# Prompt attention scored once by query rows, its probabilities transposed in blocks, in quarters of 256 queries

## What is computed

```
def fox_attend(q, fq, pq, k, v, fk, pk):
    s = einsum('bqhd,bkhd->bhqk', q, k) * (HEAD_DIM ** -0.5)
    s = s + swapaxes(fq, 1, 2)[..., :, None] - swapaxes(fk, 1, 2)[..., None, :]
    s = where(pq[:, None] >= pk[None, :], s, -inf)
    p = softmax(s, axis=-1)
    return einsum('bhqk,bkhd->bqhd', p, v)
```

## Time and profile before

| | us |
|---|---|
| median of 3 runs | 733.63 |
| lowest and highest | 733.26, 734.16 |
| the profiled execution | 732.52 |
| its span, first to last instruction | 730.8 |
| PE busy in the span | 690.2 |
| DVE, ACT, POOL busy | 414.1, 243.4, 144.4 |

### The profile page before, as it was taken

One profiled execution on the slowest core, in us unless ns is written; L12 is line 12 of the kernel. 1 busy time (PEld: TensorE's weight loads), 2 busy tenths in 40 slices (PEclk: granted clock), 3 DMA queues, 4 the chain that ended last, 5 costly groups with the idle time before them and its releaser, 6 DMA issues.

```text
span 730.8 us, 12856 instructions
## 1 busy us (share of the span) xinstructions
PE 690.2 (94%) x4958; PEld 545.2 (75%) x4958; DVE 414.1 (57%) x722; ACT 243.4 (33%) x422; POOL 144.4 (20%) x168
## 2 busy tenths in 40 slices
PE   2999999999999999999999998999998999999995
PEld 2789999888888889999999846554554232588884
DVE  4834927472353303179999953536446797455443
ACT  6636442121111345112121233444542384212211
POOL 3044112111111011213121243222320002212210
PEclk9999999999999999999999999999999999999999
DMA  8312103311110032331210687566841050032332
GB/s 256 100 37 59 29 6 67 86 32 30 31 30 2 4 80 93 104 105 30 58 29 1 187 274 252 155 201 190 270 128 54 34 188 1 1 100 73 101 115 87
DMA packets 60757, 67.27 MB, mean 92 GB/s; under 512 B 15188, under 2 KB 50907, under 8 KB 60697
## 3 DMA queue, kind: packets, MB, share of 16 engines
q1 hardware_dynamic: 55529, 51.37, 23.5%
q0 software_dynamic: 5168, 15.08, 6.9%
HBM read 57.71 MB, written 8.68 MB: 91 GB/s over the span
## 4 chain that ended last, share of the span: by engine, by line
PE 70%; DVE 20%; issue 4%; ACT 3%; SPq 2%; DMA 1%; DVEq 0%; ACTq 0%
PE PS L1727 10%; PE PS L1728 8%; PE PS L1729 8%; DVE RA L1403 8%; PE PS L1656 5%; PE PS L1655 5%; PE PS L1657 4%; PE PS L1975 3%; PE PS L1906 3%; PE PS L1992 3%; PE PS L1954 3%; PE PS L2015 3%; DVE rec L1607 2%; DVE wr L1235 1%; DVE RA L1402 1%
## 5 line engine op out<-in xcount | busy, mean ns | idle before, releaser
L1727 PE MATMUL PS<-xh,wh 128*128 128x368 f32 x576 | 202.1, 351 | 0.0
L1728 PE MATMUL PS<-xl,wh 128*128 128x368 f32 x576 | 190.0, 330 | 0.0
L1729 PE MATMUL PS<-xh,wl 128*128 128x368 f32 x576 | 189.7, 329 | 0.0
L558 POOL TENSOR_TENSOR wl<-wr,wh 128x1024 fp32r<-128x1024 f32 x24 | 61.1, 2547 | 312.1 <-ACT wh L913 312.1
L1727 PEld LDWEIGHTS PS<-xh,wh 128*128 128x128 f32 x576 | 108.2, 188 | 6.7 <-issue 1.6
L1728 PEld LDWEIGHTS PS<-xl,wh 128*128 128x128 f32 x576 | 108.3, 188 | 1.7
L1729 PEld LDWEIGHTS PS<-xh,wl 128*128 128x128 f32 x576 | 108.2, 188 | 0.0
L1235 DVE TENSOR_TENSOR wr<-wr,small 128x1024 f32<-128x1024 f32 (+1 forms) x26 | 36.1, 1388 | 45.2 <-DMA wr<-in_w_in_dram 45.1
L1538 DVE CUSTOM_DVE_ANT_0 junk<-PS,RA 128x272 bf16<-128x272 f32 (+9 forms) x84 | 39.1, 507 | 38.5 <-PE PS L1979 28.1
L1403 DVE RECIPROCAL RA<-RA 128x1104 f32<-128x1104 f32 x8 | 56.4, 7054 | 0.3
L1655 PE MATMUL PS<-woh,yh 128*128 128x512 f32 (+1 forms) x144 | 56.2, 391 | 0.0
(11 more groups left out here) (313 smaller groups left out, 1061.8 us busy)
## 6 DMA issues: line engine op xcount, KB each, us to landing
wr<-in_w_in_dram SPq DMA_DIRECT2D x24, 512.0 KB, 3.8
kpage<-in_cache_fox_k_dram SPq DMA_DIRECT2D x64, 192.0 KB, 3.8
pagesB<-in_cache_fox_v_dram POOLq DMA_DIRECT2D x32, 192.0 KB, 3.6
RA<-in_cache_fox_v_dram POOLq DMA_DIRECT2D x32, 192.0 KB, 3.9
YF<-in_x_prompt_dram SPq DMA_DIRECT2D x8, 512.0 KB, 7.1
xres<-in_x_prompt_dram SPq DMA_DIRECT2D x8, 512.0 KB, 3.9
out_y_p_dram<-zout SPq DMA_DIRECT2D x16, 256.0 KB, 2.0
wo_raw_a<-in_w_out_dram SPq DMA_DIRECT2D x6, 512.0 KB, 4.8
```

The source lines that it names most:

```text
L558: eng.tensor_tensor(low, wr[:, c % 2, :, 0:m], wh[:, c % 2, :, 0:m].bitcast(F32), ALU.subtract).then_inc(wlo_done, 1)
L1727: pe.matmul(out, high, xh[:, k, cols], start=(k == 0), stop=False)
L1728: pe.matmul(out, high, xl[:, k, cols], start=False, stop=False)
L1729: ins = pe.matmul(out, low, xh[:, k, cols], start=False, stop=(k == KT - 1))
```

## The change

The second pass is dropped. The first pass writes the scores with minus F added to SBUF (`score_rows`), and keeps them. For each tile, DVE takes the negated maximum of the row (`tile_max`, item `N`), and ACT does the exponential in place over the whole row of each head and sums it (`exps`, item `M`). The queries go in four quarters of 256. For each two blocks of keys in a quarter, PE transposes eight blocks of 128x128 probabilities of the two tiles and heads into a slot (`turn`, user `T`); the last turn of a quarter has only 16 keys. ACT copies the first turn of a quarter to `PT`, DVE the others. `attend` multiplies by the values: 256 columns for each head and block, and on the diagonal 128 and 128. DVE takes the reciprocals of the sums by query (`inverse`, item `I`), and PE spreads them to rows by a product with the identity (`inverse_rows`, item `R sum`), after which DVE multiplies.

A new `plan()` orders all this: the tiles of the next quarter are scored between the turns of this one, the exponentials come one step later, and the samples end before quarter 2 of pair 2. A list `TAIL` gives the places of `W`, `X` and the first `Y` items. `nf_cols` (L1761) goes. `kT` has one buffer instead of two, the V pages of even samples lie in `RA` and those of odd ones in `pagesB`. The V pages of sample 0 are loaded by POOL in chunk 19 of the input projection instead of behind it. The biases of pairs 1 and 2 get a buffer of their own, `nf_b`; pair 1's is loaded right behind sample 1's V pages. SP loads `w_out` from the end of `s_attend` 6 on, with waits before rows 3, 5, 6 and 7.

```diff
     s[1] = [("gate", g, t) for g in range(2) for t in range(3)]
-    s[6] = [("nf_cols",)]
+    s[6] = []
...
+    for u in scored(0, 0):
+        items, cost = score(*u)
+        steps.append((items, cost, 0.0))
+    ends = 0
+    for n_q, (p, q) in enumerate(QUARTERS):
+        if (p, q) == (2, 2):
+            ends = len(steps) + 1
+        steps.append((late, 0.0, 3.0))
+        late = []
+        ahead = scored(*QUARTERS[n_q + 1]) if n_q + 1 < len(QUARTERS) else []
+        units = turn_units(p, q)
+        behind = None
+        for n, unit in enumerate(units):
+            now, cost = [("S", ("T",) + unit)], 1.0 if n <= q else 0.4
+            if n == 0:
+                now.append(("I", (p, q)))
             if behind:
                 now.append(("V", behind))
+                cost += 1.2
+            behind = unit
+            now += late
+            late = []
+            first = 2 if q == 3 else 0
...
+        steps.append(([("V", behind), ("R", ("sum", p, q))], 1.0, 0.0))
...
+TAIL = [(1, "W", 0), (2, "W", 1), (2, "X", 0), (3, "W", 2), (3, "X", 1), (6, "X", 2), (6, "W", 3), (6, "Y", ("proj", PROJ[0])),
+        (7, "W", 4), (7, "X", 3), (7, "Y", ("proj", PROJ[1])), (8, "X", 4), (8, "W", 5), (9, "X", 5), (9, "W", 6),
+        (10, "X", 6), (10, "W", 7), (11, "X", 7)]
+EARLY_VALUES = 19
...
             for c in range(3, NCHUNK):
                 w_low(g, c)
+                if c == EARLY_VALUES:
+                    g.wait_ge(d_ptab, 16)
+                    drained(g, ("fv_rows", 7))
+                    drained(g, ("fv_rows", 8))
+                    g.wait_ge(d_k_out, 16 * 10)
+                    g.wait_ge(o_normed, 3)
+                    for i in range(3):
+                        load_values(0, i)
...
+            def exps(p, j):
+                act.wait_ge(nm_done, EI[p, j] + 1)
+                if p:
+                    act.wait_ge(inv_done, QUARTERS.index((p - 1, j // 2)) + 1)
+                for i in range(2):
+                    act.activation(score_rows(j, i), score_rows(j, i), ACT.Exp, bias=nm[:, j, i:i + 1],
+                                   accum_out=row_sum[:, j, i:i + 1]).then_inc(exp_done, 1)
...
                 for i in range(2):
-                    ins = dve.tensor_tensor_reduce(junk[:, n_ % 2, i, 0:c1 - c0], s_head(user, i)[:, 0:c1 - c0], nf_row[i][:, c0:c1],
-                                                   1.0, -3e38, ALU.add, ALU.max, pmax[:, j, i, c:c + 1])
+                    ins = dve.tensor_tensor_reduce(score_rows(j, i)[:, c0:c1], s_head(user, i)[:, 0:c1 - c0],
+                                                   nf_rows[p][i][:, c0:c1], 1.0, -3e38, ALU.add, ALU.max,
+                                                   pmax[:, j, i, c:c + 1])
...
+            def turn(user):
+                _, p, q, s = user
+                s_taken(pe, user)
+                out = s_slot(user)
...
+                for a_ in range(2):
+                    j = 2 * q + a_
+                    if s == 0:
+                        exps_done(pe, p, j)
+                    for n_, b in enumerate((2 * s, 2 * s + 1)):
+                        w = min(P, score_width(j) - P * b)
+                        for i in range(2):
+                            at = 2 * QUARTER * n_ + QUARTER * i + P * a_
+                            ins = pe.transpose(out[0:w, at:at + P], score_rows(j, i)[:, P * b:P * b + w], ident[:, :])
+                ins.then_inc(s_full, 1)
...
+                    for i in range(2):
+                        ins = add(2 * s, P, 0, 2, QUARTER * i, i, s == 0, False)
+                    for i in range(2):
+                        at = 2 * QUARTER + QUARTER * i
+                        if s < q:
+                            ins = add(2 * s + 1, P, 0, 2, at, i, False, False)
+                        else:
+                            add(2 * s + 1, NMETA, 0, 1, at, i, False, False)
+                            ins = add(2 * s + 1, P, 1, 2, at + P, i, False, False)
...
+            def inverse_rows(key):
+                _, p, q = key
+                out = ring_take(pe, key)
+                pe.wait_ge(inv_done, QUARTERS.index((p, q)) + 1)
                 for i in range(2):
+                    for a_ in range(2):
+                        ins = pe.matmul(out[64 * i:64 * i + 64, P * a_:P * a_ + P],
+                                        row_inv[:, 2 * q + a_, i:i + 1].to_broadcast([P, HD]), ident[:, :],
+                                        start=True, stop=True)
```

More of the change, by code:

```diff
@@ L146, in plan, with scored, score @@
 def plan():
-    steps = []
-    def p1_cost(j, c):
+    steps, late = [], []
+    def scored(p, q):
+        return [(p, j, c) for j, c in P1_UNITS if j // 2 == q]
+    def score(p, j, c):
         c0, c1 = p1_chunks(j)[c]
[L152 to L165, removed]
+        items = [("S", ("P1", p, j, c))]
+        if c + 1 == len(p1_chunks(j)):
+            items.append(("N", (p, j)))
+            late.append(("M", (p, j)))
+        return items, (c1 - c0) / 450 + 0.2
@@ L179, in plan @@
+            behind = unit
+            now += late
+            late = []
+            first = 2 if q == 3 else 0
+            upto = -(-len(ahead) * max(0, n + 1 - first) // max(1, len(units) - 1 - first))
+            for u in ahead[-(-len(ahead) * max(0, n - first) // max(1, len(units) - 1 - first)):upto]:
+                items, c = score(*u)
+                now += items
+                cost += c
             steps.append((now, cost, 0.0))
-    assert not soon and not later
+        steps.append(([("V", behind), ("R", ("sum", p, q))], 1.0, 0.0))
@@ L197, in plan @@
             given += 1
[L198 to L212, removed]
+        order += [(kind, key) for at, kind, key in TAIL if at == n - ends]
+    assert given == len(samples)
     for n, t in enumerate(PROJ):
@@ L2030, in max_rows @@
-            def max_rows(key):
-                out = ring_take(pe, key).bitcast(BF16)
-                pe.wait_ge(n3_done, key[1] + 1)
-                for j in range(NTILE):
-                    ins = pe.transpose(out[:, P * j:P * j + P], n3[:, j, :], identb[:, :])
+                p, q, s = unit
+                n_q = QUARTERS.index((p, q))
+                if s == 0 and n_q:
+                    pe.wait_ge(o_free, n_q)
+                turned(pe, unit)
+                pt = PT[:, TI[unit] % 3, :]
@@ L2059, in _ @@
                     top_scores(key)
-                elif kind == "S" and key[0] == "P2":
-                    key_scores(key)
+                elif kind == "S" and key[0] == "T":
+                    turn(key)
                 elif kind == "S":
```

329 lines of the change are left out of this document (134 added, 195 removed).

## The result

| | before | after |
|---|---|---|
| median of the same chips' runs, us | 733.11 (16 runs) | 739.25 (16 runs) |
| profiled execution: its time / span, us | 732.52 / 730.8 | 743.06 / 741.4 |
| ratio of the times | | 1.0083, 95% interval 1.0063 to 1.0102 |

The forecast was 732.1 us, so its sign was wrong: the kernel got slower by 6.1 us. The range, 721 to 741, holds the median.

The account below looks back on a forecast made before the run. PE's own queue was taken as the bound. PE work of -2.6 us and waits of +1.1 us summed to -1.5 us, giving 732.1 us on the median's scale (before: 733.6), range 721 to 741 us.

Parts of the forecast that it names:

- Change 3: Smaller value products on PE: 13.8 us a pair against 10.4, diagonal units at 1.33 us; +10.3 us for three pairs.
- Change 2: Added PE transposes of probability blocks: 0.90 us a full turn, 29.8 us in all.
- Change 6: PE's waits in the attention stretch: 12.5 us go and 13.6 us of new ones come, +1.1 us.
- (a): Attention's start: four exponentials precede the kT copies on ACT, so PE stops after three groups; 2.9 us, 0.5 elsewhere.
- (b): Quarters 1 and 2 of each pair: second score chunk waits for ACT's turn copy, 0.4 us eight times, 3.2 us.
- (c): Sample transposes follow their softmax with less between; PE's waits behind the sample's exp grow by 3.5 us.
- (d): At the end, X items and `wo_low` on DVE delay the copies and the projection: 3.5 us of PE waits.
- Change 5: Engine loads: DVE drops by some 26 us, ACT rises by some 23, both hidden under PE on the whole.
- Change 7: Moved loads on POOL, SP and DMA queues cost nothing; a late `w_low` in the input projection at most 2 us once.
- DVE's relief pays: PE's waits behind DVE and ACT halve to some 7 us, giving 722 us; chance 0.30.
- Exponentials become the wait: At quarter ends PE waits for maxima and exponentials, 4.3 us with hand-over, giving 741 us; chance 0.17.
- Transposes don't keep the clock up: The 30 us of added transposes lower PE's clock more often; five more dips give 740 us; chance 0.08.

Follow-up runs that it names:

- after, again: The changed kernel, unaltered, measured a second time on other chips: median 738.75 us, ratio 1.0047 to the kernel before.
- together: Against the changed kernel, all four 16-row value products of a quarter moved into the small unit: 733.34 us, ratio 0.9976 to before.
- grouped: Against the changed kernel, diagonal units do both 16-row products first, then both 128-row ones: 734.90 us, ratio 0.9989 to before.
- grouped and row by row together: Changed kernel with 16-row products first in diagonal units and the output projection waiting for `wo_low` by row: 733.17 us, ratio 0.9964 to before.
- together, row by row, with X later: Changed kernel with 16-row products only in small units, projection waiting by row, and X later in DVE's queue: 727.86 us, ratio 0.9896 to before.
- row by row: Against the changed kernel, the output projection's first tile waits for each row of `wo_low`, not all eight: 734.51 us, ratio 0.9973 to before.

## Why the prediction was wrong

**The method held: PE's queue is the bound.** DVE lost 21.3 us over the span (forecast 22 to 30) and this bought nothing on the whole, as argued. What counts is PE's sum, PE's waits and its clock. The first two came out on the wrong side: -2.6 forecast against +3.1 busy, +1.1 forecast against +3.6 idle (+1.4 and +2.3 in the profile of after, again).

**The step that failed is Change 3, the price of a diagonal value unit.** I took 0.585 for the even block and two products' worth of 0.37 for the odd one, 1.33, by a slope fitted to products that all had 128 rows and equal neighbours. From 429.88, where no wait is behind it, the unit takes 2.02 us:

```profile
429.88 2.09 PE L2012 MATMUL PS<-PT,VR 128*64 128x256 f32 x12
431.90 0.49 PE L1913 MATMUL PS<-kT,q_diag 128*32 128x344 f32 x3
```

Twelve units were forecast at 16.0 us and took 24.2, +8.3. The change of row count was left out: the unit and the small one behind it take 1.39 us from start to start in together, where no unit mixes row counts, and 2.38 in after, so the mixing costs 1.0 us a quarter, 12 us in all. That grouped comes to 1.32, close to my 1.33, is luck: my slope priced the columns some 0.3 too high (1.70 for both units against 1.39), and grouped still pays about 0.3 for two changes of row count. No unit of before mixes row counts; I gave this term no bound above 1.33, and that was the fault, since the 16-row product was in the diff.

**The transposes were mis-sized (Change 2).** 0.90 us a full turn, by the cheapest spacing of a short group, against 1.02 measured; the long run of twenty in before gives 0.12 each, and would have said 0.95:

```profile
417.15 2.44 PE L1906 MATMUL PS<-ident,kpage 128*128 128x128 f32 x20
419.52 0.73 PE L1975 MATMUL PS<-YF 64*128 64x272 f32 x4
```

Thirty full turns at 1.02 and twelve small ones at 0.31 are 34.3 us, +4.5.

**Terms that came out cheaper.** Regular value units 1.02 against 1.17: eighteen are 18.4 us, -2.7. Inverses 0.60 against 0.80: -2.4. With -0.1 for the small units the five terms add 7.6, so -2.6 becomes +5.0; the busy time shows +3.1, and +1.4 in after, again. The 2 to 4 us between stay unexplained; the removed part was not measured by itself, and the clocks are 0.97, 0.98 and 0.99.

**Waits (Change 6), one by one.** The 12.5 us named for removal were misread. By the twelve rows only 8.9 of them stand behind the prompt's exponentials, products and row maxima; 2.3 stand behind the samples' maxima (`smax`) and 1.3 behind K pages, work that the change keeps. The exponentials (4.8) and the wait for the multiplied result (2.0, L1600) went, and so did the `smax` rows; the row maxima stayed (`pmax`, 2.1 before and 2.5 after). (a) The start: 2.1 us forecast as 2.9, in its place; the first turn starts at 424.83, 8.9 us into the stretch. That is 422.2 on before's scale, forecast 422.

```profile
421.51 2.09 PE L1900 MATMUL PS<-ident,kpage 128*128 128x128 f32 x12 [2.06 <-ACT kT L1164]
...
424.83 1.57 PE L1997 MATMUL PS<-ident,rows_even 128*128 128x128 f32 x8
```

(b) The slot waits: of 0.3 to 0.5 us each, as forecast, but in eleven places and 4.2 us in all instead of eight and 3.2; the kind that I named, a score chunk behind ACT's copy, is 1.0 us of them; half of them stand behind DVE's maxima (`pmax`, 1.3 and 0.9), half behind ACT's copy of the turn (1.0 and 1.0). (c) The sample softmax: +3.7 against +3.5. (d) The end: 2.2 us at the projection and 0.4 and 0.2 ahead of it, against 3.5. The forecast came to 16.8 us of waits in all, and the twelve rows come to 19.3. Not foreseen was the 1.8 us wait for K pages, which I had said should go (0.4 in after, again). The sum also put at nothing what a new wait does to the clock: at the start of the projection some 2.3 us, the difference of 109.3 and 107.0.

**Change 5** was right on DVE's copies (1.22 us against 1.2) and wrong on ACT, which rose by 9.2 us over the span, not by 23. The group L1112 that I took out of the earlier trace rows has twelve more exponentials beside it, of 7.5 us, that write `acc`, and three copies of maxima, 3.0 us, that go as well; of the 48 reads of row sums half the time lies under the next exponential. No row of PE's waits names these exponentials; the 2.1 us at the start stand behind `kT` copies that come after them on ACT. **Change 7**, the queues, was right: no `w_low` is late in chunk 20.

**The rivals.** *DVE's relief pays* fell: waits rose instead of halving. *Exponentials become the wait* fell too, although the time is on its side: no row of PE's waits in after names an exponential of the prompt. At the end of a quarter PE goes from the inverses into the next turn without a wait (617.68 to 618.28), though I had found 4.3 us of hand-over there. *Transposes don't keep the clock up* fell: from 445 to 620 us, where most of the transposes are, the clock stands at 1.00, and it fell where PE had waited 2.19 us.

```profile
445.00:620.00 175.00, 163.83 (x1594) 101.64 (x1590) 88.38 (x305) 80.65 (x164) 30.04 (x56) 1.00 0.46 143
...
632.00:637.00 5.00, 5.00 (x12) 2.70 (x13) 0.00 (x0) 0.00 (x0) 0.00 (x0) 0.50 0.01 3
```

**The chances.** A sum of -2.6 from removed 52 and added 50 us is a small difference of large terms. A tenth off either one is 5 us, so the sign was open; a chance of 0.33 for slower was too low beside terms without a row of their own.

## What to carry to other kernels

Price a small product by its neighbours as well as by its columns: here neighbours of one row count overlapped and neighbours of different row counts hardly did. Putting the odd sizes side by side took 0.7 us off a quarter's two units, and a unit of their own 1.0. A stage that reads its operands row by row should wait row by row; a wait at its start costs more than its own length where the clock falls behind it. When PE is the bound and is made faster, expect some of the gain back as waits in the queue next to it, and look there for the next edit: against the first measurement of after, the unit and the wait alone gave 0.9 and 1.1%, both in one kernel 1.2%, and with the small products together and DVE's queue reordered 1.9%; against the second, 0.6, 0.7, 0.8 and 1.5%.

## What the runs showed of the hardware that was not expected

- Two 16-row and two 128-row products of 128 columns cost 1.5 us in alternation and 0.8 us in two pairs, though the mean record of one is the same (293 and 298 ns). With the 16-row ones moved into the small unit, its four 16-row products cost 0.58 us (609.52 to 610.10), where two had cost 0.36.
- After the wait of 2.2 us at the projection's start the products ran for some 5 us at 0.50, 1.2 GHz. In grouped and row by row together the same happened with no wait at that point, only 0.33 and 1.12 us in the 4 us before. In together, row by row, with X later, waits of 1.02 and 1.69 us in the 6 us before it were followed by nothing of the kind. Which idle time brings the fall stays open.
- The same DVE instruction on 1024 columns (`wo_low`) took 1.20 to 1.22 us in most places and 2.2 us in one or two of its eight places in the profiles of the changed kernels that were looked at: X5 in after (2.26), X3 and X4 in together, row by row, with X later. Two of PE's waits stand behind it. The cause was not looked for.
- Two dips of the clock, near 30 and 175 us, are in the profiled execution of some runs and not of others, of kernels that are alike up to there. Attention starts at 413.1 to 413.9 us where the second is missing (once, in row by row, at 416.4) and at 415.7 to 416.8 where it is there.
